# Two chained model blocks on one core: the final norm's order of work at the end of the program

## The reference, cut to what matters

```python
def rms_norm_2(x, g):
    xf = x.astype(jnp.float32)
    y = xf * lax.rsqrt(jnp.mean(xf * xf, axis=-1, keepdims=True) + EPS)
    return (y * g.astype(jnp.float32)).astype(x.dtype)
...
        h = h + conv_ffn(rms_norm_2(h, ffn_norm_g[layer]), w_up[layer], conv_w[layer], conv_b[layer],
                         w_down[layer], valid)
    return rms_norm_2(h, final_norm_g)[:, PREFIX:]
```

## Time and profile before

| | us |
|---|---|
| median of 3 runs (lowest, highest) | 2308.39 (2306.03, 2309.24) |
| the profiled execution's own time | 2305.6 |
| its span in the trace | 2303.8 |
| TensorE busy | 2241.6 (97%) |
| DVE, ACT, POOL busy | 936.0, 879.0, 1233.7 |
| from the end of the last down product to the end of the span | 17.1 |

### The profile page before, as it was taken

One profiled execution on the slowest core, in us unless ns is written; L12 is line 12 of the kernel. 1 busy time (PEld: TensorE's weight loads), 2 busy tenths in 40 slices (PEclk: granted clock), 3 DMA queues, 4 the chain that ended last, 5 costly groups with the idle time before them and its releaser, 6 DMA issues.

```text
span 2303.8 us, 31281 instructions
## 1 busy us (share of the span) xinstructions
PE 2241.6 (97%) x12283; PEld 1828.4 (79%) x12283; DVE 936.0 (41%) x1513; ACT 879.0 (38%) x1236; POOL 1233.7 (54%) x1065
## 2 busy tenths in 40 slices
PE   8999999899999989999989999999999999999998
PEld 6777777688888767777768888877888889889896
DVE  5546644511111622666551111157554236324143
ACT  4344343624324443555462423335333224222123
POOL 3665666645444565888764444455313335545552
PEclk9999999999999999999999999999999999999999
DMA  5222222222232231211222232222311213233321
GB/s 156 74 74 74 74 74 74 82 92 91 91 102 96 76 98 57 65 56 55 81 86 93 92 107 91 92 92 74 104 38 43 67 52 85 86 109 92 92 83 64
DMA packets 237958, 189.14 MB, mean 82 GB/s; under 512 B 9279, under 2 KB 228860, under 8 KB 237708
## 3 DMA queue, kind: packets, MB, share of 16 engines
q1 hardware_dynamic: 235726, 183.78, 25.9%
q10 hardware_dynamic: 2110, 3.66, 0.5%
HBM read 185.30 MB, written 2.10 MB: 81 GB/s over the span
## 4 chain that ended last, share of the span: by engine, by line
PE 86%; POOL 6%; ACT 3%; DVE 3%; issue 2%; DMA 0%; SPq 0%; DVEq 0%; ACTq 0%; POOLq 0%
PE ps L2781 44%; PE ps L3049 11%; PE ps L1396 8%; PE ps L667 4%; PE ps L2915 3%; PE ps L2823 2%; POOL hdd L448 2%; POOL hdd L446 1%; POOL w_lo L1871 1%; POOL a_lo L1892 1%; PE ps L2833 1%; PE ps L1497 1%; PE ps L735 1%; DVE xc L2476 1%; PE ps L3182 1%
## 5 line engine op out<-in xcount | busy, mean ns | idle before, releaser
L1871 POOL TENSOR_TENSOR w_lo<-raw,w_hi 128x512 fp32r<-128x512 f32 (+2 forms) x756 | 911.0, 1237 | 881.2 <-ACT w_hi L2049 880.6
L2049 ACT ACTIVATE w_hi<-raw 128x2048 fp32r<-128x2048 f32 (+2 forms) x189 | 328.5, 1739 | 529.6 <-PE ps L2781 359.0
L2781 PE MATMUL ps<-b_hi,w_hi 128*128 128x512 f32 (+1 forms) x1080 | 360.6, 359 | 2.0 <-POOL w_lo L1871 2.0
L2781 PE MATMUL ps<-b_hi,w_lo 128*128 128x512 f32 (+1 forms) x1080 | 361.9, 360 | 0.0
L2781 PE MATMUL ps<-b_lo,w_hi 128*128 128x512 f32 (+1 forms) x1080 | 360.3, 359 | 0.0
L2781 PEld LDWEIGHTS ps<-b_hi,w_hi 128*128 128x128 f32 x1080 | 193.3, 188 | 37.2 <-POOL w_lo L1871 2.5
L2781 PE MATMUL ps<-a_hi,w_lo 128*128 128x512 f32 x560 | 221.4, 395 | 0.0
L2781 PE MATMUL ps<-a_lo,w_hi 128*128 128x512 f32 x560 | 220.2, 393 | 0.0
L2781 PE MATMUL ps<-a_hi,w_hi 128*128 128x512 f32 x560 | 220.1, 393 | 0.1
L2781 PEld LDWEIGHTS ps<-b_hi,w_lo 128*128 128x128 f32 x1080 | 191.7, 188 | 32.1 <-issue 0.5
L2781 PEld LDWEIGHTS ps<-b_lo,w_hi 128*128 128x128 f32 x1080 | 192.0, 188 | 31.7
(11 more groups left out here) (416 smaller groups left out, 4237.1 us busy)
## 6 DMA issues: line engine op xcount, KB each, us to landing
raw<-in_mlp_w_dram SPq DMA_DIRECT2D x128, 512.0 KB, 4.3
raw<-in_w_up_dram SPq DMA_DIRECT2D x44, 512.0 KB, 4.9
raw<-in_ssd_w_in_dram SPq DMA_DIRECT2D x40, 512.0 KB, 4.7
raw<-in_hgrn_w_in_dram SPq DMA_DIRECT2D x48, 256.0 KB, 3.2
raw<-in_w_in_dram SPq DMA_DIRECT2D x24, 512.0 KB, 5.2
raw<-in_ssd_w_out_dram SPq DMA_DIRECT2D x16, 512.0 KB, 4.4
raw<-in_w_down_dram SPq DMA_DIRECT2D x16, 512.0 KB, 4.4
raw<-in_ple_w_gate_dram SPq DMA_DIRECT2D x12, 512.0 KB, 4.0
```

Source lines behind the costliest of these rows:

```text
L1871: last = nc.gpsimd.tensor_tensor(w_lo[:, slot, piece], raw[:, slot, i * q:(i + 1) * q], w_hi[:, slot, piece].bitcast(F32), ALU.subtract)
L2049: nc.scalar.activation(w_hi[:, slot, at:at + n], raw[:, slot, 0:n], ACT.Copy).then_inc(whi_ready, 1)
L2781: last = nc.tensor.matmul(ps[:, b + s, 0:nn], w[:, k, m * P:(m + 1) * P], v[:, k, c0 + s * nn:c0 + (s + 1) * nn], start=(k == 0 and first) ...
```

## The change

The weight is multiplied into `res` (in place) as soon as a block is finished and squared, and these unscaled blocks are transposed: blocks 0 and 1 after chunk 1 of the last four, blocks 2 and 3 after chunk 2, blocks 4 to 7 after the last tile. Block 7 is multiplied by DVE into `hv` and the others by ACT. The squares are summed with the squares as the stationary operand and one column of ones as the moving one, so that the sums lie with tokens on partitions (a 128 by 4 tile, `carried`). The token scale is then one number for each partition: for the first 512 features ACT has copied the transposed banks into `ytok` (over `xc`) before, and DVE multiplies that in place; for the last 512 ACT multiplies while it evicts the banks. SP writes four transfers of 512 KB in place of eight of 256 KB.

```diff
@@ SP
-            for n in range(2 * NCH):
-                s, c = divmod(n, NCH)
-                sp.wait_ge(ot_ready, n + 1)
-                sp.dma_start(out[0, c * P:(c + 1) * P, s * T:(s + 1) * T], otok[:, n % 4]).then_inc(s_out[n % 4], 16)
+            for c in range(NCH):
+                sp.wait_ge(acc_ready, F2T + c + 1)
+                sp.wait_ge(ot_ready, NCH + c + 1)
+                sp.dma_start(out[0, c * P:(c + 1) * P, :], ytok[:, c]).then_inc(s_out[c], 16)
@@ ACT, rms2_act
                         square2(i, k)
                         if i == 1:
                             scaled_hi(1, k)
+                        elif k < KD - 1:
+                            act.wait_ge(ln_sq, SQ2 + i * KD + k + 1)
+                            nc.scalar.activation(res[:, k, META:], res[:, k, META:], ACT.Identity,
+                                                 scale=col1(C_FIN, k)).then_inc(xc_ready, 1)
+                        if i == 2 and k == 5:
+                            act.wait_ge(ot_done, 1)
+                            for c in range(NCH):
+                                nc.scalar.activation(ytok[:, c, 0:T], bank[4 + c], ACT.Copy).then_inc(ot_ready, 1)
...
+                if i == 2:
+                    own.did(nc.scalar.activation(carried[:, 4:8], bank[tile.n % 4][:, 0:NCH], ACT.Ln, scale=1.0 / D,
+                                                 bias=lneps[:, 1:2]))
+                    own.wait()
+                    nc.scalar.activation(carried[:, 0:4], carried[:, 4:8], ACT.Exp, scale=-0.5).then_inc(rstd_ready, 1)
+                    return
@@ ACT, end of block2_act
-            for n in range(2 * NCH):
-                act.wait_ge(ot_done, n + 1)
-                if n >= 4:
-                    act.wait_ge(s_out[n % 4], 16)
-                nc.scalar.activation(otok[:, n % 4], bank[n % 6], ACT.Copy).then_inc(ot_ready, 1)
+            act.wait_ge(rstd_ready, 7)
+            act.wait_ge(ot_done, 2)
+            for c in range(NCH):
+                nc.scalar.activation(ytok[:, c, T:D], bank[4 + c], ACT.Identity, scale=carried[:, c:c + 1]).then_inc(ot_ready, 1)
@@ DVE, end of block2_dve (rms2_dve and its 8 products are gone)
-            rms2_dve(C_FIN)
+            dve.wait_ge(free_dve, fd())
+            nc.vector.tensor_scalar(hv[:, 0], res[:, KD - 1, META:], col1(C_FIN, KD - 1), None,
+                                    ALU.mult).then_inc(g_lo, 1)
+            dve.wait_ge(rstd_ready, 7)
+            for c in range(NCH):
+                dve.wait_ge(ot_ready, c + 1)
+                nc.vector.tensor_scalar(ytok[:, c, 0:T], ytok[:, c, 0:T], carried[:, c:c + 1], None,
+                                        ALU.mult).then_inc(acc_ready, 1)
@@ TensorE, block2_pe
+            def to_tokens(k):
+                src = hv[:, 0] if k == KD - 1 else res[:, k, META:]
+                for c in range(NCH):
+                    last = nc.tensor.transpose(bank[4 + c][:, k % 4 * P:(k % 4 + 1) * P], src[:, c * P:(c + 1) * P], ident)
+                return last
+
+            def token_squares():
+                b = bank[tile.n % 4]
...
+                for c in range(NCH):
+                    cols = slice(META + c * P, META + (c + 1) * P)
+                    nc.tensor.matmul(b[:, c:c + 1], sq[:, 0, cols], ones[:, 0:1], start=True, stop=False)
+                    last = nc.tensor.matmul(b[:, c:c + 1], sq[:, sq_slot(KD - 1), cols], ones[:, 0:1], start=False, stop=True)
...
                 for j in range(4):
                     chunk_mm(j % 2, nt, 256, (a_hi, a_lo), fd, ...)
+                    if last and j in (1, 2):
+                        pe.wait_ge(xc_ready, 7 * KD + 2 * j)
+                        to_tokens(2 * j - 2)
+                        done = to_tokens(2 * j - 1)
+                        if j == 2:
+                            done.then_inc(ot_done, 1)
...
-            ffn(6)
-            rms2_pe(2)
-
-            for s in range(2):
...
+            ffn(6, last=True)
+            pe.wait_ge(ot_ready, NCH)
+            pe.wait_ge(xc_ready, 8 * KD - 1)
+            for k in range(4, KD - 1):
+                to_tokens(k)
+            token_squares()
+            pe.wait_ge(g_lo, 2 * KD + 1)
+            to_tokens(KD - 1).then_inc(ot_done, 1)
```

More of the change, by code:

```diff
@@ L301, in two_blocks @@
         acc = sb("acc", [P, T], F32, hid)
-        otok = hv
+        ytok = xc[:].rearrange("p k n -> p (k n)")[:, 0:NCH * D].rearrange("p (c d) -> p c d", c=NCH)
         hid.close()
@@ L866, in block2_sync @@
             ffn(6, 2048)
-            for n in range(2 * NCH):
-                s, c = divmod(n, NCH)
-                sp.wait_ge(ot_ready, n + 1)
-                sp.dma_start(out[0, c * P:(c + 1) * P, s * T:(s + 1) * T], otok[:, n % 4]).then_inc(s_out[n % 4], 16)
+            for c in range(NCH):
+                sp.wait_ge(acc_ready, F2T + c + 1)
+                sp.wait_ge(ot_ready, NCH + c + 1)
+                sp.dma_start(out[0, c * P:(c + 1) * P, :], ytok[:, c]).then_inc(s_out[c], 16)
             for s in s_out:
-                sp.wait_ge(s, 2 * 16)
+                sp.wait_ge(s, 16)
         def block2_pool(pool, chunk, pub, b_at, cut_lo):
@@ L1111, in block2_act @@
             rms2_act(2, FD_END - KD)
-            for n in range(2 * NCH):
-                act.wait_ge(ot_done, n + 1)
-                if n >= 4:
-                    act.wait_ge(s_out[n % 4], 16)
-                nc.scalar.activation(otok[:, n % 4], bank[n % 6], ACT.Copy).then_inc(ot_ready, 1)
-        def block2_dve(dve, tile, fd, own, pub, b_at, add_square, scaled_lo):
[L1119 to L1124, removed]
+            act.wait_ge(rstd_ready, 7)
+            act.wait_ge(ot_done, 2)
+            for c in range(NCH):
+                nc.scalar.activation(ytok[:, c, T:D], bank[4 + c], ACT.Identity, scale=carried[:, c:c + 1]).then_inc(ot_ready, 1)
+        def block2_dve(dve, tile, fd, own, pub, b_at, add_square, scaled_lo):
             b0 = b_at()
@@ L1716, in block2_pe, with ffn @@
             b_at.add(4)
-            def ffn(nt, first=False):
+            def to_tokens(k):
[5 more added lines that the diff above has]
+                b = bank[tile.n % 4]
+                pe.wait_ge(free_dve, fd(-3))
+                pe.wait_ge(q_sum, Q_AT[4] + 18)
+                pe.wait_ge(ln_sq, sq_at(KD))
+                for c in range(NCH):
+                    cols = slice(META + c * P, META + (c + 1) * P)
+                    nc.tensor.matmul(b[:, c:c + 1], sq[:, 0, cols], ones[:, 0:1], start=True, stop=False)
+                    last = nc.tensor.matmul(b[:, c:c + 1], sq[:, sq_slot(KD - 1), cols], ones[:, 0:1], start=False, stop=True)
+                last.then_inc(sq_used, KD)
+                sq_at.add(KD)
+            def ffn(nt, first=False, last=False):
                 mark = (fa.n, fd.n - 1)
```

## The result

| | before | after |
|---|---|---|
| median of 20 runs (lowest, highest), us | 2307.49 (2305.26, 2309.72) | 2311.18 (2308.99, 2313.38) |
| span of the profiled execution, us | 2303.8 | 2311.0 |
| start of ACT's copy of the last chunk to T7, us | 16.67 | 25.34 |
| T7 (end of the last down product) to the end of the span, us | 17.10 | 11.86 |

The ratio is 1.0016, with a 95% interval of 1.001 to 1.0022: 3.7 us more, inside the 0.2% that the prediction called no change, on the side that it named. The interval excludes no difference at all, and its upper end lies just above the 0.2%.

What follows compares the result with a forecast made beforehand. It took T7's time on TensorE and the tail behind it as the bound: + 4.35 + 1.75 + 2.3 - 6.2 = +2.2 us on the three-run median 2308.39, giving 2310.6 us, range 2305.5 to 2314.

Steps and rivals of the forecast that it cites:

- rival 1: TensorE's clock holds at full rate through the new wait behind tile 3; time 2308.3 us, chance 0.16.
- sixteen transposes ahead of T7: Transposes of blocks 0 to 3 on TensorE before T7, at 0.11 us each: 1.75 us more.
- the wait behind tile 3: TensorE stalls between tiles 3 and 4 for ACT's blocks 0 and 1: 4.35 us, between 4.15 and 4.5.
- half clock behind it: After the wait TensorE works at 1.2 GHz for about 5.1 us, losing 2.3 us, between 1.5 and 3.1.
- tail: From T7 to the span's end: shrinks from 17.1 to 10.9 us, 6.2 us less.
- The chain copy, square, product, square, product: ACT's work from the last chunk's copy through blocks 0 and 1, ending at 2274.08, TensorE going on at 2274.12.
- The second wait: TensorE's wait for blocks 2 and 3 behind tile 5: costs nothing, over 8 us covering under 3 of ACT work.
- in which it stays low up to the tail: Rival 2: TensorE's clock stays low behind the new wait; 2314.7 us if for 14 us; chance 0.12.
- in which the wait does not arise: Rival 3: ACT squares blocks 0 and 1 ahead of the last chunk's copy, so no wait; 2303.9 us, chance 0.07.
- the price of the sums: In the tail, eight one-column products take 1.08 us, ending at T7 + 2.5; 1.3 later at the 264-column price.
- first issue: In the tail, the first output transfer is issued at T7 + 3.75, after eviction and product of about 0.7 each.
- The choice to take the best rate: Output transfers in the tail: 2.10 MB at 393 GB/s takes 5.34 us, rather than 6.4 at 327.

Runs made afterwards that it cites:

- the kernel without the wait: Changed kernel, but ACT squares and scales blocks 0 and 1 before its copy of the last chunk; median 2304.16 us, ratio 0.9988 to before.
- the kernel kept busy: Changed kernel, but TensorE makes 18 unused products behind tile 3, ahead of its wait for ACT; median 2307.82 us, ratio 1.0001 to before.
- the run with half the sums: ACT squares and scales blocks 0 and 1 before its last chunk's copy, and the four products adding block 7's squares are left out; one run, 2303.61 us.

## Why the prediction was right, and by how much each step was off

The forecast was + 2.2 us; the traces give + 3.43 and the medians + 3.69. That the forecast time, 2310.6, lies only 0.6 from the measured 2311.18 is partly luck: it was built on the median of three runs, 2308.39, which is 0.9 above that of twenty, and this made up for much of the 1.5 that the sum fell short. The range of 2305.5 to 2314 also takes in the time of rival 1 (2308.3), so it is the trace, and not the time, that bears out the mechanism. The experiments split it: what differs between the kernel without the wait and before, between the kernel kept busy and the one without the wait, and between the changed kernel and the one kept busy, are the first three terms.

| term | predicted us | measured us | from |
|---|---|---|---|
| sixteen transposes ahead of T7 | + 1.75 | + 1.74 | 18.41 - 16.67 |
| the wait behind tile 3 | + 4.35 | + 4.43 | 22.84 - 18.41 |
| half clock behind it | + 2.3 | + 2.50 | 25.34 - 22.84 |
| tail | - 6.2 | - 5.24 | 11.86 - 17.10 |
| sum | + 2.2 | + 3.43 | 37.20 - 33.77 |

**The wait** came at the place, on the instruction and for the reason named: the transposes of blocks 0 and 1 (L1735) waited for ACT's L939. The chain copy, square, product, square, product was forecast from the earlier trace rows to within 0.1 us. **The second wait**, behind tile 5, did not arise; its eight transposes cost 0.79 us.

**The clock** fell, as behind the waits of the earlier trace rows; the 5.3 us at 1.2 GHz lie next to the mean of 5.1. Products 0.427 apart in place of 0.232 lose 0.456 of each us, 2.4 us in all; the run that kept TensorE busy gives 2.50. The rivals in which the clock holds, in which it stays low up to the tail, and in which the wait does not arise are all three excluded, by the stretches of 2276.8 to 2283.1 and of 2283.2 to 2299.1 and by the wait's own row.

**The tail** is the term that was mis-sized: 11.86 us instead of 10.9. The step that failed is the price of the sums: "The nearest row, eight of 32 columns, takes 1.08, so they end at +2.5". The eight records of that row are four products: its line issues one for each of four token blocks, and each leaves two records, as the one-column products here do. Read so, four products of 32 columns take 1.08 where four of one column took 1.02 (the run with half the sums), and eight would have been put at a little under twice 1.08, where 1.92 was measured. (The four records of 264 columns in the earlier trace rows are two products as well.) The sums also begin at +1.55 instead of +1.40. Before, the first two products waited for DVE's sum alone and only the other two for ACT's last square; now all eight wait for both, and the first starts 0.14 behind the end of the square. Its weight load starts 0.11 behind that end (the row of PEld above), so the load itself fills little of the 0.14; what fills it stays open. With both, the sums end at +3.47, and Ln, Exp and the first eviction follow in 0.59: the scale meets the data at +4.06, where +3.0 was forecast. Removing four of the eight products shortened the tail by 0.91, so the whole of this stands on the path.

From there on the forecast held: first issue 0.77 behind the eviction's start (0.75 forecast), first data 0.83 later (0.86), the transfers 5.2 us (5.34), the end 1.0 after them (0.98). The Trainium skill, page "DMA: Bandwidth & Descriptors", section "Bandwidth", under "Where 436 GB/s comes from", has a core's HBM share of about 358 GB/s limit such transfers, by which the writes would take an estimated 5.9 us. The trace does not agree: 403 GB/s over the whole 5.2 us of the output. The Trainium skill's page "Perfetto Trace Analysis", section "Engine Utilization", under "Roofline", has it otherwise: the figure is a core's share while both cores of a pair use the memory, and a core alone may reach some 120% of it. The trace agrees with that, at 113% (403 / 358), for a program on one core.

The choice to take the best rate of the earlier trace rows rather than its mean of 327 GB/s was right: once the four transfers are queued, the dips are gone.

Two sums in the prediction do not come out of the numbers beside them, without consequence: 2308.3 - 2.4 is 2305.9 and not 2305.5, and eight records at the price of 264 columns take 2.3 us, 1.2 more than 1.08 and not 1.3.

## What to carry to other kernels

Before an engine's stream is made to wait for another engine at an inner place, read what stands ahead of the awaited work in that engine's order: here a copy that itself waits for TensorE stood there, and 6.9 us in which the work could have been done lay idle just before it. The wait on TensorE cost its length, 4.4 us, and then 2.5 us for the work behind it at half clock, together more than the 5.2 us that the shorter tail gave; moving two squares and two products ahead of the copy, or the transposes one chunk later, turned a slightly slower kernel into one that is 0.12% to 0.18% faster. When a row is used as a price, count how many instructions of the program its records are.

## What the runs showed of the hardware that was not expected

- A product of float32 operands in the sums leaves two weight loads and two records, and with one moving column the next follows after 0.22 us. From the first record to the last, four products take 1.02 us with one column and 1.08 with 32: at these widths the number of columns hardly matters.
- The output in four transfers with rows of 4 KB moved at 403 to 406 GB/s, with single slices up to 471; in eight with rows of 2 KB, also queued without gaps, at 380 to 382. Single slices depend on their width and should not be compared: the transfers of before reach 393 in the slices of a quarter of a us of the earlier trace rows, but 420 in slices of 0.2 us.
- The granted clock fell while TensorE was still waiting (0.50 from 2276.8, work again from 2277.9), and the tail, which ran at 0.50 before, ran at 1.00 in the changed kernel, where transposes and sums follow the last product with gaps of a quarter of a us at most.
